# The rotary part of latent attention: contraction over 32 partitions in place of 128 zero-padded ones

## The reference, cut to what matters

```python
def one_block(args):
    ql, qr, qc = args
    s = (jnp.einsum('bhqc,bkc->bhqk', ql, k_lat) + jnp.einsum('bhqr,bkr->bhqk', qr, k_rope)).astype(jnp.float32) * MLA_SCALE
    s = jnp.where(k_chunk[None, :] <= qc[:, None], s, NEG_INF)
    p = jax.nn.softmax(s, axis=-1).astype(k_lat.dtype)
    return jnp.einsum('bhqk,bkc->bhqc', p, k_lat)
```

## Time and profile before

| | before |
|---|---|
| median of three runs | 1479.53 us (1478.79 to 1483.79) |
| time of the profiled execution | 1478.79 us |
| its span in the trace | 1477.0 us |
| PE busy | 1401.9 us (95%) |
| DVE busy | 634.6 us (43%) |
| ACT busy | 349.6 us (24%) |
| POOL busy | 49.5 us (3%) |
| HBM traffic over the span | 294 GB/s |
| mean granted clock of PE | 0.962 |

### The profile page before, as it was taken

The page is one execution under the profiler, slowest core; times in us unless marked ns, Lnnn a source line. Parts: engine busy times, 40 slices in busy tenths (PEclk is TensorE's granted clock), DMA queues, the critical chain, the costliest instruction groups (busy, mean ns, idle before and its releaser), DMA issues.

```text
span 1477.0 us, 17801 instructions
## 1 busy us (share of the span) xinstructions
PE 1401.9 (95%) x6519; PEld 738.6 (50%) x6519; DVE 634.6 (43%) x1267; ACT 349.6 (24%) x722; POOL 49.5 (3%) x78
## 2 busy tenths in 40 slices
PE   6999889899999999999999779999999999999994
PEld 4565564654544454445444366544454455445442
DVE  0554562733433434343333567333443344343436
ACT  1441340322221222222222231212221222122211
POOL 5200100100000000000000110000000000000000
PEclk9996599899999999999999979999999999999997
DMA  9203020759998998999898923599899989989971
GB/s 291 74 6 115 8 93 0 279 207 373 392 390 361 394 392 347 420 378 391 364 402 346 384 75 130 235 389 376 345 421 389 381 361 413 384 367 390 396 294 32
DMA packets 63622, 435.21 MB, mean 295 GB/s; under 512 B 4323, under 2 KB 6435, under 8 KB 13536
## 3 DMA queue, kind: packets, MB, share of 16 engines
q1 hardware_dynamic: 60800, 427.08, 72.1%
q0 software_dynamic: 2784, 7.62, 1.7%
HBM read 432.93 MB, written 1.76 MB: 294 GB/s over the span
## 4 chain that ended last, share of the span: by engine, by line
PE 92%; DVE 5%; issue 1%; ACT 1%; DMA 0%; SPq 0%; DVEq 0%
PE bank L850 30%; PE bank L766 24%; PE bank L798 15%; PE bank L792 12%; PE bank L750 4%; PE bank L860 1%; PE bank L920 1%; PE bank L1026 1%; PE bank L907 1%; DVE sb_x L1520 1%; PE bank L1023 1%; DVE sb_x L1516 1%; PE bank L1165 1%; PE bank L1019 1%; DVE sb_ln_st L1512 1%
## 5 line engine op out<-in xcount | busy, mean ns | idle before, releaser
L1449 DVE TENSOR_TENSOR sb_x<-sb_x,bank 128x512 f32<-128x512 f32 (+1 forms) x396 | 242.1, 679 | 118.6 <-PE bank L792 118.6
L798 PE MATMUL bank<-sb_wslot,sb_ht 128*64 128x512 f32 x1024 | 231.0, 593 | 0.0
L850 PE MATMUL bank<-sb_wslot,sb_xg_own 128*64 128x512 f32 x1024 | 226.5, 595 | 1.7 <-ACT sb_xg_own L1217 1.7
L850 PE MATMUL bank<-sb_wslot,sb_xt 128*64 128x512 f32 x1024 | 226.8, 595 | 0.0
L1468 DVE TENSOR_TENSOR sb_hh<-sb_sg,bank 128x256 f32<-128x256 f32 x64 | 27.0, 422 | 376.7 <-ACT sb_sg L1241 376.7
L1455 DVE SCALAR_TENSOR_TENSOR sb_yl<-bank,sb_gslot,sb_yh 128x512 fp32r<-128x512 f32 x128 | 96.1, 751 | 162.6 <-ACT sb_yh L1223 162.6
L766 PE MATMUL bank<-sb_pick,sb_xh 128*128 128x512 f32 x432 | 160.8, 401 | 0.9 <-DVE sb_x L1818 0.9
L792 PE MATMUL bank<-sb_yh,sb_place 128*128 128x512 f32 x396 | 157.5, 398 | 3.3 <-DVE sb_yl L1455 3.3
L792 PE MATMUL bank<-sb_yl,sb_place 128*128 128x512 f32 x396 | 156.6, 395 | 0.0
L1241 ACT ACTIVATE sb_sg<-bank 128x256 f32<-128x256 f32 x64 | 24.6, 384 | 550.1 <-PE bank L850 550.1
L798 PEld LDWEIGHTS bank<-sb_wslot,sb_ht 128*64 128x64 f32 x1024 | 72.8, 137 | 144.5 <-issue 139.3
(11 more groups left out here) (298 smaller groups left out, 1156.8 us busy)
## 6 DMA issues: line engine op xcount, KB each, us to landing
sb_wslot<-in_moe_w_gate_dram SPq DMA_DIRECT2D x64, 2048.0 KB, 8.3
sb_wslot<-in_moe_w_up_dram SPq DMA_DIRECT2D x64, 2048.0 KB, 12.9
sb_wslot<-in_moe_w_down_dram SPq DMA_DIRECT2D x64, 2048.0 KB, 15.2
sb_w_in_hi<-in_w_in_dram SPq DMA_DIRECT2D x2, 2048.0 KB, 24.0
sb_w_in_lo<-in_w_out_dram SPq DMA_DIRECT2D x1, 4096.0 KB, 13.2
sb_w_in_lo<-in_w_in_dram SPq DMA_DIRECT2D x2, 1024.0 KB, 10.4
sb_ln_g<-in_ln_g_dram POOLq DMA_DIRECT2D x4, 512.0 KB, 4.4
sb_ln_b<-in_ln_b_dram POOLq DMA_DIRECT2D x4, 512.0 KB, 5.8
```

The lines of the kernel that those rows point to most:

```text
L798: last = pe.matmul(y_b[c][64 * e:64 * e + 64, :], ht[:, k, 64 * e:64 * e + 64], w_down[u][:, e, k * D + c * 512:k * D + (c + 1) * 512], st ...
L850: last = pe.matmul(gu_b[64 * e:64 * e + 64, :], xgt[b][:, k, sl], w_gu[u][:, :, e, k * FE:(k + 1) * FE], start=k == 0, stop=k == DK_SLICES ...
L1449: dve.tensor_tensor(dst, dst, banks.tile[order[f]][0:rows, :], ALU.add).then_inc(s["added"], 1)
```

## The change

The rotary operands are cut to the 32 partitions that mean something: the tiles `kr_t` and `skr_t` have 32 partitions, and the queries are read from partitions 0 to 31. The rotary product contracts over 32 partitions. The memset of `kr_t` goes, and `ZEROED` is one less; the memset of `skr_t` stays but covers 32 partitions. All other edits rewrite slices that name the same data.

```diff
-ZEROED = 2 + 9 + 3
+ZEROED = 2 + 9 + 2
...
-        q_few_rot = hi["q_few_rot"]
+        q_few_rot = hi["q_few_rot"][0:ROPE, :]
...
-        kr_t = mb("kr_t", [P, T_COLS])
+        kr_t = mb("kr_t", [ROPE, T_COLS])
         skv_t = mb("skv_t", [P, S_KEYS])
-        skr_t = mb("skr_t", [P, S_KEYS])
+        skr_t = mb("skr_t", [ROPE, S_KEYS])
...
-            gp.memset(kr_t[:, :], 0.0).then_inc(zeroed, 1)
...
-                        ql, qr = q_lat[:, hs[0], q0:q0 + nq], q_rot_t[:, hs[0], q0:q0 + nq]
+                        ql, qr = q_lat[:, hs[0], q0:q0 + nq], q_rot_t[0:ROPE, hs[0], q0:q0 + nq]
...
-                act.activation(kr_t[0:ROPE, cols], ps[0:ROPE, 384:384 + rows], ACT.Copy).then_inc(banks.empty_sem(n), 1)
+                act.activation(kr_t[:, cols], ps[0:ROPE, 384:384 + rows], ACT.Copy).then_inc(banks.empty_sem(n), 1)
```

More of the change, by code:

```diff
@@ L1329, in _ @@
                 act.activation(skv_t[:, g * P:g * P + rows], ps[:, 0:rows], ACT.Copy)
-                act.activation(skr_t[0:ROPE, g * P:g * P + rows], ps[0:ROPE, P:P + rows], ACT.Copy).then_inc(banks.empty_sem(n), 1)
+                act.activation(skr_t[:, g * P:g * P + rows], ps[0:ROPE, P:P + rows], ACT.Copy).then_inc(banks.empty_sem(n), 1)
             copy(uk_t[:, :, :], ("ukT",), lambda ps: ps[:, :].rearrange("p (g n) -> p g n", g=4))
@@ L1342, in _ @@
             act.activation(skv_t[:, SAMPLE0:], kv_t[:, SAMPLE0:], ACT.Copy)
-            act.activation(skr_t[0:ROPE, SAMPLE0:], kr_t[0:ROPE, SAMPLE0:], ACT.Copy)
+            act.activation(skr_t[:, SAMPLE0:], kr_t[:, SAMPLE0:], ACT.Copy)
             act.activation(past[own, 2, :], ckv_n[own, 2, :], ACT.Copy).then_inc(skeys_ready, 1)
@@ L1364, in _ @@
                 banks.copied(act, ("qrT", i))
-            for src, dst in ((q_lat, q_few), (q_rot_t[0:ROPE, :, :], q_few_rot[0:ROPE, :])):
+            for src, dst in ((q_lat, q_few), (q_rot_t[0:ROPE, :, :], q_few_rot)):
                 for c0, q0, nq in ((0, 2 * P, TAIL), (MH * TAIL, SAMPLE0, N_DEC)):
```

## The result

| | before | after |
|---|---|---|
| median | 1481.19 us (1478.79 to 1483.79, 4 runs) | 1508.49 us (1506.62 to 1512.25, 4 runs) |
| profiled execution | 1478.79 us, span 1477.0 | 1507.37 us, span 1505.6 |
| mean granted clock of PE | 0.962 | 0.942 |

The change makes the kernel slower: ratio 1.0179, 95% interval 1.0165 to 1.0193, about 27 us. The forecast was 1502.8 (+23.3), between 1483 and 1508; on the 1479.53 us against which it was made, the ratio gives 1506.0. The changed kernel's own median, 1508.49, lies 0.5 above the range; the fourth run of the kernel before moved its median up by 1.7 too.

A forecast was written before the change was run, and what follows sets the result against it. The prediction took the chain of waits, 92% PE, to bound the kernel. Terms of +1.2, +20.1 and +2 us summed to +23.3: 1502.1 on the profiled execution, 1502.8 on the median, range 1483 to 1508.

The forecast's parts named there:

- the one that was put first: Attention: added switches of partition count, and PE at half clock from 164.5 us to its end; +23.3 us, 62%.
- The memset and the product: Dropping the kr_t memset (0.39 us of POOL) and contracting the 38 rotary matmuls over 32 partitions: no gain.
- The switch: Around each rotary product, PE finishes and loads weights unhidden: entry 0.30 us at half clock, 0.19 at full; exit 0.25.
- The exit into transposes: From the 32-row rotary product to the probability transposes: 0.25 us taken, between 0.13 at half clock and 0.30.
- The clock: The larger term: few-partition work and added pauses keep PE at half clock from 164.5 us to the attention's end.
- The stage ahead: 133.8 to 157.7 us: PE busy 20.95 of 23.90 us over 64 partitions and fewer, clock at half throughout.
- +1.2 to pt(6): Attention up to block 6's transposes, half clock in both kernels: switches add 1.2 us (1.0 to 1.4).
- +20.1 for the five pairs: Attention between the transposes of blocks 6 and 16: 43.9 us at half clock against 23.76, +20.1 (19 to 20.7).
- the third, "+2 (1 to 3.5)": From block 16's transposes to the linear attention's transposes, 6.0 us before: +2 us, as the clock may rise midway.
- The clock does as before: Rival: the clock rises as in the kernel before, only the switches count: +4.0 us, 1483.5 us; 14%.
- The one of no cost for the switch: Rival: changing partition count around the rotary product costs nothing, so not slower, 1479.5 us; 7%.
- An earlier rise: Rival: the clock rises at 168 us in place of 185, making the kernel faster, 1477.2 us; 5%.

The follow-up runs named there:

- the fillers: Unread 128-row products ahead of the even attention blocks' transposes, added to the changed kernel (1480.3 us) and to the kernel before (1476.0 us).
- rotary first: The changed kernel with its two score products swapped, the 32-row rotary product ahead of the latent one: 1500.0 us, ratio 1.0133 to the kernel before.
- the tiny product: The kernel before with one 8-column product over 32 zero partitions between the two score products: 1496.6 us, ratio 1.0119.
- the twin: The kernel before with unread 128-row products ahead of the transposes of the even blocks 0 to 14: 1476.0 us, ratio 0.9971.
- one filler: Eight unread 128-row products before the first transposes, added to the changed kernel (1508.5 us) and to the kernel before (1481.7 us).
- e11_after_fillers: The changed kernel with unread 128-row products ahead of the transposes of the even blocks 0 to 14: 1480.3 us, ratio 1.0012 to the kernel before.

## Why the prediction was right, and where it was off

The mechanism is the one that was put first, and it was right in sign and nearly in size. The two terms that were off cancel in part, which is luck: the loop was put 0.9 us too high and what lies behind it 3.9 too low.

- *The memset and the product.* Nothing gained: the second record of a rotary pair is 0.66 us long at half clock over 32 rows as over 128.
- *The switch.* Entry at half clock as forecast from ol: the last latent matmul of block 5 starts at 184.35, the second rotary one, which has its load hidden, at 185.56.

```profile
184.35 0.66 PE L765 MATMUL bank<-sb_kv_t,sb_w_in_hi 128*128 128x272 f32 x1
...
185.56 0.66 PE L765 MATMUL bank<-sb_kr_t,sb_w_in_hi 32*128 32x272 f32 x1
```

That is 1.21 us for two steps of 0.453, so 0.30. The exit into transposes, for which no row stood, comes to 0.13 of finishing (185.56 to 186.14 is 0.58) and 0.06 of load: about 0.19 against the 0.25 taken, inside its bounds. This explains the pair: 7.21 and twice 0.30 and 0.19 make 8.19, less the load that the 7.21 held already; measured 8.13, forecast 8.31. The Trainium skill's sentence that a change of tiling mode drains the engine (TensorEngine Tiling, Key Properties) agrees with these 0.13 us of finishing. Its sentence that a product over 32 rows takes the time of one over 128 (TensorE: Matmul & The Clock Gate, the table on why this matters) holds for the product, 0.66 us and 0.66, and misses the kernel by 27 us.
- *The clock.* At half from 164.5 to beyond the attention, as forecast. That it was the larger part is shown by the fillers: with the clock held up the change costs 4.4 to 6 us, so 21 to 23 of its 27 are clock. That few rows alone suffice is shown by rotary first. The other half of the forecast's reading, that pauses keep the clock down too, isn't shown: the tiny product's trace has the rise at the same place in the work, and only the mean clock of its two slower executions speaks for it. The stage ahead was read not quite rightly: from 133.8 to 157.7 us 12 of the 52 records, those of `qe_t`, are over 128 partitions. A better row was in the same trace, with all but three of its instructions over 64 partitions:

```profile
110.00:120.00 10.00, 10.00 (x126) 7.28 (x124) 4.35 (x8) 0.76 (x2) 0.00 (x0) 0.50 0.01 2
```

PE is busy all of these 10 us at half clock, and the rise came at 123.6, in the transposes over 128 partitions behind it.
- *The sum.* +1.2 to pt(6) measured 1.1; +20.1 for the five pairs measured 19.2. The term that was mis-sized is the third, "+2 (1 to 3.5)" for the time behind pt(16): 3.1 us up to the transposes of `og`, inside its bounds, and 2.8 more behind them. The sum ended where the attention does, at 216.98, and took it that the clock would rise in the midst. It rose at 247.7, after transposes and the value products had run at half clock too. On the sum this makes 5.9 in place of 2, and that is most of the difference to the measured 27.
- *The rivals.* "The clock does as before", +4.0, has become an experiment: 4.4 to 6 against the twin. The one of no cost for the switch is refuted by the rows above. An earlier rise wasn't seen in any run of the change by itself.

What stays open is the exact rule. Few-row work keeps the clock from rising; how much of it is needed, whether the added pauses take part, and whether 64 rows count for more than 32, these runs don't tell.

## What to carry to other kernels

A zero-padded contraction can be worth its zeros: a product over 32 rows took as long as one over 128, and each change of the number of rows between products in a stream cost 0.14 to 0.30 us here. Look first at PEclk stage by stage: where a stage runs near the edge between the two clocks, a small change that adds few-row work can cost many times its own price (here 21 to 23 us by the clock to 4 to 6 by itself), and the other way round, padding the short last tile of a loop gained 0.5%. Extend such a sum to the place where the clock comes back, not to the end of the stage.

## What was not expected of the hardware

- Once few rows hold the clock at half, the added switches cost their own time and no more: the attention took 77.0 us with rotary first and 82.3 with the change, which has two entries and two exits a pair more.
- Waits and few rows do different things. Behind a wait of 1.19 to 1.34 us the clock fell in the runs with one filler, with 128 rows as with 32, though behind one of 0.96 us in `e11_after_fillers` it did not; only without the 32 rows did it come back within the attention. With full-row fillers mixed in, the changed kernel stayed at 1.00 from 169.6 us on.
- The kernels do the same at their start, but the first projection's pace differs between executions: from 19.0 to 22.4 us there are 14 matmuls in the before trace and 7 in that of the changed kernel with one filler, and the attention's first product starts at 158.1 us in the one and at 162.6 in the other. That the clock's first rise came at another moment is a reading; PEclk doesn't show it there. Two single profiles that are compared differ by such amounts before the change has done anything.
